# A mixture-of-experts kernel in which four experts are loaded by number, one ring slot is left free for the routed order, and the second pair of experts runs as group 12 of 22

## The chip, the cores and the metric

The kernel runs on one core of a Trainium2 chip. Its time is the device time in microseconds of one execution, and the figure that stands for it is the median of several runs. Five engines work beside each other: TensorE (PE in the profile, with PEld for its weight loads), VectorE (DVE), ScalarE (ACT), GpSimd (POOL) and SyncE (SP), which here issues nearly all loads from memory. They wait for one another by counting semaphores.

## The reference, cut to what matters

A network of two layers works on 256 tokens of width 1024, in float32. The first layer mixes the tokens by attention and a state space model, the second by a long convolution. Each ends in the same mixture of experts, which is the stage that the change touches:

```
def moe(h, router_w, router_b, w_gate, w_up, w_down, sh_gate, sh_up, sh_down):
    scores = jax.nn.sigmoid(jnp.einsum('td,de->te', xf, router_w, preferred_element_type=jnp.float32))
    _, idx = lax.top_k(scores + router_b.astype(jnp.float32), TOP_K)
    sel = jnp.take_along_axis(scores, idx, axis=-1)
    wts = sel / jnp.sum(sel, axis=-1, keepdims=True) * ROUTE_SCALE
    ...
        hid = jax.nn.silu(xb @ w_gate[e]) * (xb @ w_up[e])
        return (hid @ w_down[e]) * w[:, None].astype(xb.dtype)
    ...
    shared = (jax.nn.silu(xf @ sh_gate) * (xf @ sh_up)) @ sh_down
    return (routed + shared).reshape(B, L, Dm)
```

There are 64 experts, each with an inner width of 256; every token goes to its 6 best ones. An expert's weights are 3 MB: 2 MB of gate and up, 1 MB of down. The shared expert, as large as one of the others, sees all tokens. So a layer reads 65 x 3 MB of expert weights, whatever the routing.

## The kernel before

**Columns and groups.** The 64 experts of a layer are worked through in an order that the router computes on the chip, by how many tokens each expert got. A place in this order is a *column*. Columns are put together in 22 groups (`NG`). A group is a pair, two experts of up to 64 tokens each, or a triple, one of up to 64 and two of up to 32. The rows of a group fill the 128 partitions. Groups 0 and 1 are pairs, groups 2 to 21 triples. The code counts triples by `t = n - 2` (`TRIPLES` is 20). What goes beyond these places is done by a loop at the end, which isn't entered here.

**Experts by number.** The order is known only when the router's logits, the choice of six and the counts are through. So that weights can be loaded meanwhile, five experts (`FIXED = STATIC + 1`) stand in columns 0 to 4 by number, whatever their load: DVE overwrites their place in the ranking. `first_experts` loads them ahead of the order.

**The ring.** SBUF holds six slots of 3 MB (`RING`). Column c uses slot `(c + 3) % 6` (`slot_of`), so the slot of column c is freed by the group of column c - 6 (`group_of`). Slot 2 (`SHARED`) first holds the shared expert, and column 5 takes it over. The down weights of columns 5 and 11 go to a tile of their own (`down_aside`).

**Loads.** `moe_loads` (line 570) is SyncE's program for a stage. SyncE waits for the first `tables_ready`, reads expert numbers out of the order table (`expert_at`, line 577), and issues loads (`load`, line 507), each behind a wait on the slot. The semaphores are `sh_gu` (shared expert's gate and up products, one count for each half of them), `gu_front` (the first half of a group's gate and up products), `gu_mm` (all of them) and `dn_mm` (the down products). SyncE issues in program order, so a wait holds back every later load. Loads come in three forms:

- pieces of 1 MB (front half of gate and up, back half, down) for triples 0, 1, 2 and the last,
- gate and up in one load, then down, for triples 3 to 7 and 18 (group 20),
- whole experts of 3 MB for triples 8 to 17:

```
            def whole(t):

                return LATE <= t < TRIPLES - 2
```

A whole expert waits for `dn_mm`; its gate and up can't come ahead of its down weights.

**The work on PE.** `moe_pe` first turns out the logits, then the routing's small matmuls with the shared expert's gate and up products between them (`shared_gate_up(0)` to `(3)`), and then the loop over the 22 groups. A group is: gate and up products (`gate_up_of`), scatter of the group before (`filler`), picking of the next group's rows (`pick_rows`), transposition, down products (`down_of`). Down products signal `dn_mm`, which frees the group's slots. The group's gate and up products wait for its loads. In the profile these matmuls have line 778, that of a helper. Matmuls of 128 x 512 float32 are gate and up or down products, those of 128 x 256 bfloat16 the scatter.

**The order on DVE.** The order table is evicted from PSUM by one operation (line 2011) that needs the second count of `route_mm`. That count is put on the last of three matmuls, of which only the first writes the order.

Of the kernel before, what the change touches and what calls it, by code (L numbers as in the profile page):

```python
# [38 lines left out]
FIXED = STATIC + 1  # L39
PAIRS = STATIC // 2  # L40
NG = PAIRS + (NE - STATIC) // 3
BIG = STATIC + NG - PAIRS
TRIPLES = NG - PAIRS
# [47 lines left out]
def columns_of(n):  # L91

    if n < PAIRS:
        return [(2 * n, slice(0, S)), (2 * n + 1, slice(S, 2 * S))]
    c = STATIC + 3 * (n - PAIRS)
    return [(c, slice(0, S)), (c + 1, slice(S, S + HALF)), (c + 2, slice(S + HALF, 2 * S))]
# [7 lines left out]
def group_of(c):  # L104
    return c // 2 if c < STATIC else PAIRS + (c - STATIC) // 3

# [19 lines left out]
def program(nc, A):  # L126
# [8 lines left out]
    with ExitStack() as ctx:  # L135
# [182 lines left out]

        def w_down(slot, f, c):
            a = 2 * KD * FF + f * D + c * 512  # L320
            return wring[:, slot, a:a + 512]

        def down_aside(c):

            return c % RING == SHARED + RING - FIRST_SLOT and c < 2 * RING
# [5 lines left out]
        def slot_of(e):  # L331
            return (e + FIRST_SLOT) % RING

        def whole(t):

            return LATE <= t < TRIPLES - 2

        def picked_ahead(n):

            return LATE < n - PAIRS < TRIPLES - 1  # L340

        def split_gate_up(c):

            return RING <= c < STATIC + 9

        def down_loads(t, li):

            def loads(last):
                return sum(0 if whole(i) else 2 if i == 0 else 3 for i in range(t % 2, last + 1, 2))
            return li * loads(TRIPLES - 1) + loads(t)  # L350

        def triple_loads(t, li):

            def loads(last):
                return sum(2 if split_gate_up(c) else 1 for i in range(t % 2, last + 1, 2)
                           for c in range(STATIC + 3 * i, STATIC + 3 * i + 3) if c >= FIXED)
            return li * loads(TRIPLES - 1) + loads(t)

# [146 lines left out]
        def _(sp):  # L505
# [54 lines left out]

            def first_experts(li, experts):
                for e in experts:
                    load(wring[:, slot_of(e)], A["w_experts"][li, e], f"w_pair{min(e // 2, 1)}")
# [6 lines left out]
            def moe_loads(li):  # L570
# [3 lines left out]
                first_experts(li, (3, 4))  # L574
# [6 lines left out]
                def gate_up_part(columns, experts, t, front):  # L581
                    for c in columns:
                        n = group_of(c - RING)
# [5 lines left out]
                        name = "w_back" if t == TRIPLES - 1 and not front else f"w_gu{t % 2}"  # L589
                        load(wring[:, slot_of(c), part], A["w_experts"][li, experts[c]][:, part], name)  # L590

                def half_loads(columns, experts, t, down):
                    part, name = (slice(GUW, WEXP), f"w_dn{t % 2}") if down else (slice(0, GUW), f"w_gu{t % 2}")
                    for c in columns:
                        if c - RING >= 0:
                            sp.wait_ge(sem("dn_mm" if down else "gu_mm"), li * (DOWNS if down else NG) + group_of(c - RING) + 1)
                        else:
                            sp.wait_ge(sem("sh_gu"), 2 * (li + 1))
                        if down and down_aside(c - RING) and not down_aside(c):
# [6 lines left out]
                for front in (True, False):  # L606
                    gate_up_part((6,), first, 0, front)
                    gate_up_part((7,), first, 1, front)
                half_loads((6,), first, 0, True)
                half_loads((7,), first, 1, True)  # L610
                gate_up_part((8, 9), first, 1, True)
                gate_up_part((8, 9), first, 1, False)
                half_loads((8, 9), first, 1, True)
                for t in range(2, NG - PAIRS):
                    triple = range(STATIC + 3 * t, STATIC + 3 * t + 3)
                    experts = {c: expert_at(c) for c in triple}
                    if t in (2, TRIPLES - 1):
                        gate_up_part(triple, experts, t, True)
                        gate_up_part(triple, experts, t, False)
                        half_loads(triple, experts, t, True)  # L620
                        continue
                    if whole(t):
                        for c in triple:
                            sp.wait_ge(sem("dn_mm"), li * DOWNS + group_of(c - RING) + 1)
                            load(wring[:, slot_of(c)], A["w_experts"][li, experts[c]], f"w_gu{t % 2}")
                        continue
                    half_loads(triple, experts, t, False)
                    half_loads(triple, experts, t, True)
# [14 lines left out]
            load(wring[:, SHARED], A["w_shared"][0], "w_shared")  # L643
# [42 lines left out]
            load(wring[:, SHARED], A["w_shared"][1], "w_shared")  # L686
# [89 lines left out]
        def _(pe):  # L776
# [316 lines left out]
            def moe_pe(li):  # L1093
# [59 lines left out]
                pe.wait_ge(sem("w_shared"), 16 * (li + 1))  # L1153
                def shared_gate_up(c, ks=range(KD)):
                    for k in ks:
                        last = mm(ps[:, 6 + c // 2, (c % 2) * L:(c % 2 + 1) * L], gate_up(SHARED, k)[:, c * P:(c + 1) * P], hX[:, k], k == 0, k == KD - 1)
# [31 lines left out]
                mm(ps[0:1, 2, 2 * P:2 * P + NE], mcst("tok", 0, 1), sorting[:, 0:NE], True, True)  # L1188
# [3 lines left out]
                last.then_inc(sem("route_mm"), 1)  # L1192
                pe.wait_ge(sem("route"), 4 * (li + 1))
# [10 lines left out]
                def shared_part(n, last):  # L1204

                    ks = ((0,), (1,)) if n == 0 else ((2, 3), (4,)) if n == 3 else ((5, 6), (7,)) if n == 4 else ((), ())
# [5 lines left out]
                for n in range(NG):  # L1212
                    t = n - PAIRS
# [4 lines left out]
                    if t < 0:  # L1218
                        pe.wait_ge(sem(f"w_pair{n}"), 16 * (2, 3)[n] * (li + 1))
                    else:  # L1220
# [463 lines left out]
        def _(dve):  # L1684
# [258 lines left out]
            def moe_dve(li):  # L1943
# [5 lines left out]
                ch(dve.tensor_copy(rank_at[:, 0:STATIC], mcst("iota", 0, STATIC)))  # L1949
                placed = rank_at[:, STATIC:].rearrange("p (g m) -> p g m", m=3)  # L1950
                ch(dve.tensor_copy(placed[:, :, 0], mcst("iota", STATIC, BIG - STATIC)))
# [35 lines left out]
                dve.wait_ge(sem("route_mm"), 3 * li + 1)  # L1987
# [5 lines left out]
                ch(ts(loads[:, 0:FIXED], mcst("iota", 0, FIXED), -1.0, 1e6, M, AD))  # L1993
# [8 lines left out]

                ch(tt(ahead, counts, folded, M))
# [6 lines left out]
                dve.wait_ge(sem("route_mm"), 3 * li + 2)  # L2010
                ch.then(ts(order, ps[0:1, 2, 2 * P:2 * P + NE], -1.0, None, AD), "tables_ready")
                by_rank = ps[:, 2, 0:2 * P].rearrange("p (t n) -> p t n", t=2)
                ch(dve.tensor_copy(pos, by_rank[:, :, 0:NE]))
                ch(dve.tensor_copy(rt[:, :, :, 1], by_rank[:, :, NE:]))

# [3 lines left out]
                def one_hots(q):  # L2019
                    a, b = max(SG * q, PAIRS), min(SG * (q + 1), NG)  # L2020
                    if q == 0:
                        ch(tt(selg[:, :, 0:PAIRS].rearrange("p t g (h s) -> p t (g h) s", h=2), mcst("iota").unsqueeze(1).unsqueeze(1).broadcast_to([P, 2, STATIC, S]),
                              pos[:, :, 0:STATIC].unsqueeze(3).broadcast_to([P, 2, STATIC, S]), ALU.is_equal))
# [9 lines left out]
                def tables(q):  # L2033
# [6 lines left out]
                    if a < PAIRS:  # L2040
                        ch(dve.tensor_reduce(wtab[S + HALF:, a:PAIRS], tab[S + HALF:, 0:PAIRS - a, NR + 1:2 * NR], AX.X, AD))
                    t = max(a, PAIRS)
                    ch.then(dve.tensor_reduce(wtab[S + HALF:, t:b], tab[S + HALF:, t - a:, 2 * NR + 1:3 * NR], AX.X, AD), "tables_ready")

                def hot_columns(n):

                    c = columns_of(n)[0][0]
                    if n < PAIRS:
                        tt(hot[n % 2].rearrange("p t (h s) -> p t h s", h=2), mcst("iota").unsqueeze(1).unsqueeze(1).broadcast_to([P, 2, 2, S]),
                           pos[:, :, c:c + 2].unsqueeze(3).broadcast_to([P, 2, 2, S]), ALU.is_equal).then_inc(sem("hot_ready"), 1)  # L2050
                        return
                    ch(tt(hot[n % 2][:, :, 0:S], mcst("iota").unsqueeze(1).broadcast_to([P, 2, S]), pos[:, :, c:c + 1].broadcast_to([P, 2, S]), ALU.is_equal))
                    tt(hot[n % 2][:, :, S:].rearrange("p t (h s) -> p t h s", h=2), mcst("iota", 0, HALF).unsqueeze(1).unsqueeze(1).broadcast_to([P, 2, 2, HALF]),
# [385 lines left out]
```

## Time and profile before

| | us |
|---|---|
| median of 3 runs | 1430.07 |
| lowest and highest of them | 1428.53, 1432.94 |
| profiled execution, its own time | 1428.19 |
| its span from the first to the last instruction | 1426.3 |
| PE busy in the span | 1270.1 (89%) |
| DVE busy | 610.4 (43%) |
| ACT busy | 273.4 (19%) |

The span is 1.9 shorter than the execution's own time, since that also holds what lies around the instructions. Times in the rows below count from the span's start. Queue 1, which carries nearly all loads, had packets under way for 87.0% of what 16 DMA engines could have had. In the rows, an engine's busy time says that it had an instruction in work, not that it was at its peak. A wait ends with the one that released it, given behind an arrow.

### The profile page before, as it was taken

To read this page: it belongs to the slowest core of one execution; us is meant where nothing else is said; L and a number is where in the kernel's file an instruction comes from. 1 tells how busy PE (TensorE), PEld (TensorE's weight loads), DVE (VectorE), ACT (ScalarE), POOL (GpSimd) and SP (SyncE) were. 2 spreads that over 40 slices of the span, in tenths; PEclk is the share of its full clock that TensorE was granted. 3 is DMA by queue.
4 is the path that set the end of the run, shared out by engine and by line. 5 is a ranking of instruction groups with operands and counts; after the bars stand their busy time and mean duration, and the time that the engine had idled before them with its cause. 6 is when DMAs were issued, how large, how long until landed. Compare 5 with 4: busy or idle time off the path is not lost.

```text
span 1426.3 us, 23074 instructions
## 1 busy us (share of the span) xinstructions
PE 1270.1 (89%) x9704; PEld 729.9 (51%) x9704; DVE 610.4 (43%) x1131; ACT 273.4 (19%) x464; POOL 60.2 (4%) x112
## 2 busy tenths in 40 slices
PE   5999988999998878888899999999999778978887
PEld 1445435775554444454446767875555334443444
DVE  5898872254432222222224687863433212221222
ACT  3226341321111111111112113131111101110111
POOL 0010581000000000000000000000000000000000
PEclk9999999999999999999998999999999989999999
DMA  9664775969999999999998962588999999999996
GB/s 379 230 215 89 161 203 208 411 252 397 422 425 420 428 428 428 427 428 428 425 418 310 380 263 102 227 347 332 397 423 422 421 431 424 425 429 429 421 421 274
DMA packets 53899, 502.84 MB, mean 353 GB/s; under 512 B 9692, under 2 KB 16604, under 8 KB 20188
## 3 DMA queue, kind: packets, MB, share of 16 engines
q1 hardware_dynamic: 53244, 499.18, 87.0%
q8 instruction: 80, 1.31, 0.4%
q10 hardware_dynamic: 544, 2.10, 0.4%
q14 instruction: 31, 0.25, 0.1%
HBM read 496.57 MB, written 4.69 MB: 351 GB/s over the span
## 4 chain that ended last, share of the span: by engine, by line
PE 52%; DMA 35%; DVE 9%; SPq 2%; issue 1%; ACT 1%; DVEq 0%; ACTq 0%
PE ps L778 49%; DMA arena<-in_w_experts 29%; DMA arena<-in_ada_w 6%; SPq L507 2%; PE ps L460 2%; ACT arena L1436 1%; DVE arena L2248 1%; DVE arena L2238 1%; DVE arena L2237 1%; DVE arena L2156 0%; DVE arena L1889 0%; PE ps L831 0%; DVE arena L2236 0%; DVE arena L1902 0%; PE ps L1043 0%
## 5 line engine op out<-in xcount | busy, mean ns | idle before, releaser
L778 PE MATMUL ps<-arena 128*32 128x512 f32 (+10 forms) x9192 | 1214.3, 456 | 138.4 <-DMA arena<-in_w_experts 55.8
L778 PEld LDWEIGHTS ps<-arena 128*32 128x32 f32 (+6 forms) x9192 | 698.5, 139 | 642.9 <-issue 492.1
L1436 ACT ACTIVATE arena<-ps 128x512 f32<-128x512 f32 (+6 forms) x261 | 142.1, 544 | 932.4 <-PE ps L778 886.2
L2098 DVE SCALAR_TENSOR_TENSOR arena<-arena,ps 128x256 f32<-128x256 f32 x44 | 21.1, 481 | 270.0 <-ACT arena L1436 270.0
L1436 ACT ACTIVATE arena<-arena 128x256 f32<-128x256 f32 (+7 forms) x143 | 93.8, 681 | 154.1 <-DVE arena L2116 58.2
L2114 DVE CAST arena<-ps 128x512 bf16<-128x512 f32 x42 | 29.0, 691 | 164.0 <-PE ps L778 164.0
L2058 DVE COPY arena<-ps 128x512 f32<-128x512 f32 x44 | 30.4, 691 | 138.7 <-PE ps L778 138.7
L2086 DVE TENSOR_TENSOR arena<-arena 128x1024 bf16<-128x1024 f32 x42 | 51.5, 1225 | 37.3 <-ACT arena L1436 37.0
L2116 DVE TENSOR_TENSOR arena<-ps,arena 128x1024 f32<-128x1024 f32 x42 | 51.4, 1224 | 1.4
L768 POOL MEMSET arena<- 128x1 f32 x2 | 0.2, 100 | 1168.4 <-PE ps L778 1168.4
L460 PE MATMUL ps<-arena 128*24 128x512 f32 x256 | 33.0, 614 | 3.2 <-DMA arena<-in_ada_w 3.2
L2106 DVE COPY arena<-ps 128x256 f32<-128x256 f32 x44 | 18.5, 422 | 28.6 <-PE ps L1096 28.6
L1436 ACT ACT_TABLE_LOAD x15 | 19.2, 1283 | 23.5 <-DVE arena L2170 11.5
L1436 ACT ACTIVATE arena<-ps,arena 128x512 f32<-128x512 f32 (+3 forms) x29 | 17.0, 585 | 35.2 <-DVE arena L1903 20.6
L2248 DVE SCALAR_TENSOR_TENSOR arena<-arena 128x512 f32<-128x512 f32 x28 | 21.1, 752 | 1.0
L1043 PE MATMUL ps<-arena 128*128 128x128 f32 x64 | 11.0, 299 | 8.4 <-DVE arena L1908 8.2
L1043 PEld LDWEIGHTS ps<-arena 128*128 128x128 f32 x64 | 8.0, 151 | 19.0 <-DVE arena L1908 15.4
L460 PEld LDWEIGHTS ps<-arena 128*24 128x24 f32 x256 | 6.5, 104 | 21.3 <-issue 16.0
L2094 DVE TENSOR_SCALAR arena<-arena 128x256 bf16<-128x256 f32 (+1 forms) x44 | 15.2, 346 | 0.1
L1902 DVE TENSOR_REDUCE arena<-ps 128x1 f32<-128x512 f32 x16 | 11.1, 691 | 8.1 <-PE ps L778 7.8
L2236 DVE TENSOR_SCALAR arena<-arena 128x256 f32<-128x256 f32 x20 | 8.3, 414 | 12.2 <-ACT arena L1436 11.5
L725 POOL TENSOR_TENSOR arena<-arena 128x64 f32<-128x64 f32 (+4 forms) x20 | 10.4, 518 | 57.9 <-ACT arena L1436 56.4
(233 smaller groups left out, 471.6 us busy)
## 6 DMA issues: line engine op xcount, KB each, us to landing
arena<-in_w_experts SPq DMA_DIRECT2D x70, 3072.0 KB, 22.2
arena<-in_w_experts SPq DMA_DIRECT2D x98, 1024.0 KB, 15.0
arena<-in_w_experts SPq DMA_DIRECT2D x38, 2048.0 KB, 21.6
arena<-in_ada_w SPq DMA_DIRECT2D x34, 1024.0 KB, 6.7
arena<-in_ada_w SPq DMA_DIRECT2D x7, 2048.0 KB, 19.4
arena<-in_hy_w_in SPq DMA_DIRECT2D x6, 2048.0 KB, 15.1
arena<-in_w_shared SPq DMA_DIRECT2D x2, 3072.0 KB, 10.5
arena<-in_hy_w_out SPq DMA_DIRECT2D x1, 4096.0 KB, 12.1
```

What stands on the lines that cost most here:

```text
L460: last = pe.matmul(ps[32 * k:32 * k + 2 * GROUP, 7, :], scz[:, 4 * half + k, a:a + 2 * GROUP], w[:, k], start=i == first and half == 0, st ...
L507: sp.dma_start(dst, src).then_inc(sem(name), 16)
L778: return pe.matmul(out, lhsT, rhs, start=start, stop=stop, skip_group_check=skip)
L1043: last = pe.transpose(ps[:, 2 + n % 2, k * P:(k + 1) * P], prob[:, n % 3, k * P:(k + 1) * P], ident)
L1436: return act.activation(out, in_, func, **kw)
L2058: dve.tensor_copy(xgT[n % 2][:, 4:8].rearrange("p k t -> p (k t)"), ps[:, DN + 1, :]).then_inc(sem("xt_dve"), 1)
L2086: tt(yb[:, 2], yr, yb[:, 1], SU).then_inc(sem("y_dve"), 1)
L2098: stt(hh, sg, wtab[:, n:n + 1], ps[:, GU, FF:2 * FF], M, M).then_inc(sem("h_done"), 1)
L2106: dve.tensor_copy(hT2.rearrange("p f t -> p (f t)"), ps[:, HT, 0:2 * P]).then_inc(sem("hT_ready"), 1)
L2114: ch(dve.tensor_copy(yb[:, 0, 0:512], ps[:, DN, :]))
L2116: tt(yr, ps[:, DN:DN + 2, :].rearrange("p b n -> p (b n)"), yb[:, 0], SU).then_inc(sem("y_dve"), 1)
L2248: ins = ts(ada_sums[n], w, c, None, M) if half == 0 and k == 0 else stt(ada_sums[n], w, c, ada_sums[n], M, AD)
```

## The change

Four experts stand by number instead of five, and they stand in columns 0, 1, 2 and 5. Column 3, the first by order, has slot 1, which nothing occupies; column 4 takes over the shared expert's slot, and does so in two halves. Group 0 is a pair, groups 1 to 11 are triples, group 12 (`MIDDLE`) is the second pair (columns 62 and 63), groups 13 to 21 are triples again. `t = n - 1` now counts all groups behind the first, so `LAST` is 20. The slots follow from a table, and `FREED_BY` says which group was the last to use a column's slot.

The shared expert's gate and up arrive as two loads, so that the first two quarters of its products use one half of the slot and the others the second; each partition reads its rows in runs of 256 elements. Its products behind the routing are put in another order, and parts of its down products move to groups 2 and 3. The order table is evicted as soon as its own matmul is through. `whole` now goes up to the last group but one.

The core of the diff:

```diff
-FIXED = STATIC + 1
-PAIRS = STATIC // 2
-NG = PAIRS + (NE - STATIC) // 3
+FIXED_COLUMNS = (0, 1, 2, 5)
+TRIPLES = (NE - 4) // 3
+NG = TRIPLES + 2
+LAST = TRIPLES
+MIDDLE = 12
...
+def slots_of(n):
+
+    if n in (0, MIDDLE):
+        return (FIRST_SLOT, FIRST_SLOT + 1) if n == 0 else (0, FIRST_SLOT)
+    if n < MIDDLE:
+        return (0, 3, 4) if n % 2 == 0 else (5, 1, SHARED)
+    return (0, 3, 1) if n % 2 == 0 else (5, 4, SHARED)
+
+
+SLOT, GROUP_OF, FREED_BY = {}, {}, {}
+for n in range(NG):
+    for slot, (c, _) in zip(slots_of(n), columns_of(n)):
+        FREED_BY[c] = max((GROUP_OF[b] for b in SLOT if SLOT[b] == slot), default=None)
+        SLOT[c], GROUP_OF[c] = slot, n
...
-            return LATE <= t < TRIPLES - 2
+            return LATE <= t < LAST
...
+            def shared_load(li):
+                halves = A["w_shared"][li][:, 0:2 * KD * FF].rearrange("p (k h n) -> p h k n", k=KD, h=2)
+                for h in range(2):
+                    load(wring[:, SHARED, h * KD * FF:(h + 1) * KD * FF].rearrange("p (k n) -> p k n", n=FF), halves[:, h], "w_shared")
+                load(wring[:, SHARED, 2 * KD * FF:], A["w_shared"][li][:, 2 * KD * FF:], "w_shared")
...
-                first_experts(li, (3, 4))
+                first_experts(li, (3,))
...
-                first = {c: expert_at(c) for c in range(FIXED, STATIC + 6)}
-                half_loads((5,), first, 0, False)
-                half_loads((5,), first, 0, True)
...
+                first = {3: expert_at(3)}
+                half_loads((3,), first, 0, False)
+                first[4] = expert_at(4)
+                half_loads((3,), first, 0, True)
+                for n, part in enumerate((slice(0, FRONT), slice(FRONT, GUW))):
+                    sp.wait_ge(sem("sh_gu"), 2 * li + n + 1)
+                    load(wring[:, SHARED, part], A["w_experts"][li, first[4]][:, part], "w_gu0")
+                half_loads((4,), first, 0, True)
+                for t in range(1, LAST + 1):
+                    columns = [c for c, _ in columns_of(t + 1) if c not in FIXED_COLUMNS]
+                    experts = {c: expert_at(c) for c in columns}
+                    if t in (1, 2, 3, LAST):
...
             sp.wait_ge(sem("y_mm"), 1)
-            load(wring[:, SHARED], A["w_shared"][0], "w_shared")
+            shared_load(0)
...
-                mm(ps[0:1, 2, 2 * P:2 * P + NE], mcst("tok", 0, 1), sorting[:, 0:NE], True, True)
+                mm(ps[0:1, GU, 0:NE], mcst("tok", 0, 1), sorting[:, 0:NE], True, True).then_inc(sem("route_mm"), 1)
...
-                shared_gate_up(2)
                 pick_rows(0)
+                shared_gate_up(3, range(0, 4))
+                shared_gate_up(3, range(4, KD)).then_inc(sem("sh_gu"), 1)
                 find_tokens(0)
-                shared_gate_up(3).then_inc(sem("sh_gu"), 1)
...
+                dve.wait_ge(sem("route_mm"), 4 * li + 2)
+                ch.then(ts(order, ps[0:1, GU, 0:NE], -1.0, None, AD), "tables_ready")
+                dve.wait_ge(sem("route_mm"), 4 * li + 3)
```

Three places in the order of instructions. The first is SyncE's program in the first layer, from the router's last constants (`in_mcst`) to the first loads by order. A row gives the line, the operation, what is written and read, and the semaphore waited for; `ISA` carries a wait or the address, `TENSOR_LOAD` reads an entry of the order. Before:

```order
L507 DMA arena<-in_mcst 128x389
L507 DMA arena<-in_w_experts 128x6144 x2
L577 TENSOR_LOAD arena [waits tables_ready]
...
L577 TENSOR_LOAD arena
L577 ISA x2
L507 ISA [waits sh_gu]
L507 DMA arena<-in_w_experts 128x4096
L507 ISA [waits sh_gu]
L507 DMA arena<-in_w_experts 128x2048
L507 ISA [waits gu_front]
```

Now:

```order
L526 DMA arena<-in_mcst 128x389
L526 DMA arena<-in_w_experts 128x6144
L602 TENSOR_LOAD arena [waits tables_ready]
L602 ISA x2
L526 ISA
L526 DMA arena<-in_w_experts 128x4096
L602 TENSOR_LOAD arena
L602 ISA x2
L526 ISA
L526 DMA arena<-in_w_experts 128x2048
L526 ISA [waits sh_gu]
L526 DMA arena<-in_w_experts 128x2048
```

Before, five entries are read and then `sh_gu` stands ahead of the first load; now one entry is read and the 2 MB load behind it has no wait but the table's. The `sh_gu` wait stands two loads later.

The second place is again SyncE's program, at the loads of group 20, the last but one of the stage, three experts. Before:

```order
L507 ISA [waits gu_mm]
L507 DMA arena<-in_w_experts 128x4096
L507 ISA [waits gu_mm]
L507 DMA arena<-in_w_experts 128x4096
L507 ISA [waits gu_mm]
L507 DMA arena<-in_w_experts 128x4096
L507 ISA [waits dn_mm]
L507 DMA arena<-in_w_experts 128x2048
```

Now:

```order
L526 ISA [waits dn_mm]
L526 DMA arena<-in_w_experts 128x6144
L526 ISA [waits dn_mm]
L526 DMA arena<-in_w_experts 128x6144
L526 ISA [waits dn_mm]
L526 DMA arena<-in_w_experts 128x6144
```

Three loads of gate and up ahead of three of down have become three of whole experts, which wait for the down products of the group before in their slots. The third place is DVE's program from the sorting matrix (64 x 64) to the copies of the token places (128 x 128). Before:

```order
L2000 TENSOR_SCALAR arena<-arena 64x64 [waits dve_chain] x2
L2003 TENSOR_TENSOR arena<-ps,arena 128x64 [waits route]
...
L2008 TENSOR_TENSOR arena<-arena 128x1 [waits dve_chain]
L2011 TENSOR_SCALAR arena<-ps 1x64 [waits route_mm,route]
L2013 COPY arena<-ps 128x128 [waits tables_ready]
```

Now:

```order
L2023 TENSOR_SCALAR arena<-arena 64x64 [waits dve_chain] x2
L2030 TENSOR_TENSOR arena<-arena 128x256 [waits route]
L2039 TENSOR_SCALAR arena<-ps 1x64 [waits route_mm]
L2042 COPY arena<-ps 128x128 [waits route_mm,tables_ready]
```

The order's eviction (1 x 64) now comes ahead of the operations on counts, and a selection for group 0 (128 x 256) stands ahead of it.

## Rows read from the trace of the kernel before

**Rows 1.** The page: GB/s in 40 equal slices of the span

```profile
GB/s 379 230 215 89 161 203 208 411 252 397 422 425 420 428 428 428 427 428 428 425 418 310 380 263 102 227 347 332 397 423 422 421 431 424 425 429 429 421 421 274
```

**Rows 2.** Windows: us, busy PE, PEld, DVE, ACT, POOL, PEclk, DMA share, GB/s

```profile
960.00:968.00 8.00, 8.00 (x60) 7.45 (x60) 5.65 (x17) 0.60 (x1) 0.00 (x0) 1.00 0.00 0
444.00:754.00 310.00, 261.43 (x2176) 136.99 (x2173) 76.09 (x124) 36.92 (x57) 0.10 (x1) 0.94 1.00 426
```

**Rows 3.** The page: the chain that ended last, by engine

```profile
PE 52%; DMA 35%; DVE 9%; SPq 2%; issue 1%; ACT 1%; DVEq 0%; ACTq 0%
```

**Rows 4.** SyncE: order reads (durations in ns, starts in us) and first ordered loads

```profile
L577 SPq TENSOR_LOAD <-arena x5: 261/273/485, 299.9 to 302.4; - x5
...
310.96 0.37 SPq L507 DMA_DIRECT2D arena<-in_w_experts  x1
...
968.60 0.35 SPq L507 DMA_DIRECT2D arena<-in_w_experts  x1
```

**Rows 5.** Timeline around the order: start, duration, instruction, [idle before <-releaser]

```profile
298.66 0.09 PEld L778 LDWEIGHTS ps<-arena 128*1 128x1 f32 x2 [0.33 <-issue]
...
299.68 0.21 DVE L2011 TENSOR_SCALAR arena<-ps 1x64 uint32<-1x64 f32 x1 [0.66 <-PE ps L778]
```

**Rows 6.** The chain that ended last: start, duration, step

```profile
592.09 30.22 DMA arena<-in_w_experts
...
637.70 28.68 DMA arena<-in_w_experts
...
1341.96 27.30 DMA arena<-in_w_experts
...
1383.23 1.46 SPq L507
...
1387.07 26.95 DMA arena<-in_w_experts
```

**Rows 7.** Loads issued at 318.50, 344.98 and 327.39; issue to landing

```profile
arena<-in_w_experts SPq DMA_DIRECT2D x1, 1024.0 KB, 13.7
...
arena<-in_w_experts SPq DMA_DIRECT2D x1, 1024.0 KB, 5.6
...
327.39 0.33 SPq L507 DMA_DIRECT2D arena<-in_w_experts  x1
...
arena<-in_w_shared SPq DMA_DIRECT2D x2, 3072.0 KB, 10.5
```

**Rows 8.** PE's timeline, end of the first layer's stage

```profile
725.21 12.96 PE L778 MATMUL ps<-arena 128*32 128x512 f32 x116 [0.86 <-DMA arena<-in_w_experts]
738.11 7.83 PE L778 MATMUL ps<-arena 128*128 128x256 bf16 x70
...
748.56 7.64 PE L778 MATMUL ps<-arena 128*32 128x512 f32 x52 [2.61 <-DMA arena<-in_w_experts]
756.14 8.04 PE L778 MATMUL ps<-arena 128*128 128x256 bf16 x54
```

**Rows 9.** PE's timeline, end of the second layer's stage

```profile
1369.31 9.39 PE L778 MATMUL ps<-arena 128*32 128x512 f32 x84 [0.94 <-DMA arena<-in_w_experts]
...
1414.16 7.29 PE L778 MATMUL ps<-arena 128*32 128x512 f32 x48 [0.88 <-DMA arena<-in_w_experts]
```

**Rows 10.** Windows (columns as in rows 2) and PE's timeline at 1169.81

```profile
748.60:753.90 5.30, 5.30 (x33) 1.30 (x34) 0.00 (x0) 0.00 (x0) 0.00 (x0) 0.68 1.03 428
1169.80:1179.60 9.80, 9.79 (x65) 2.42 (x66) 0.00 (x0) 0.00 (x0) 0.00 (x0) 0.72 0.98 415
...
1169.81 12.11 PE L778 MATMUL ps<-arena 128*32 128x512 f32 x84 [7.17 <-DMA arena<-in_w_experts]
```

**Rows 11.** Window (columns as in rows 2) over the load of w_in

```profile
32.00:38.00 6.00, 4.30 (x28) 1.61 (x26) 4.50 (x2) 0.60 (x1) 0.00 (x0) 1.00 1.05 380
```

**Rows 12.** The router's constants (issued at 277.86; KB, us to landing), first routing product

```profile
arena<-in_mcst SPq DMA_DIRECT2D x1, 194.5 KB, 4.1
...
282.21 3.98 PE L778 MATMUL ps<-arena 128*64 128x256 f32 x16 [1.34 <-ACT arena L1436]
```

More of the change, by code:

```diff
@@ L329, in w_down_of, with slot_of @@
             return at(a, 512) if down_aside(c) else w_down(slot_of(c), f, half)
-        def slot_of(e):
-            return (e + FIRST_SLOT) % RING
+        def slot_of(c):
+            return SLOT[c]
         def whole(t):
-            return LATE <= t < TRIPLES - 2
+            return LATE <= t < LAST
         def picked_ahead(n):
-            return LATE < n - PAIRS < TRIPLES - 1
+            return LATE < n - 1 < LAST
         def split_gate_up(c):
-            return RING <= c < STATIC + 9
+            return c == 4 or RING <= c < 14
         def down_loads(t, li):
             def loads(last):
-                return sum(0 if whole(i) else 2 if i == 0 else 3 for i in range(t % 2, last + 1, 2))
-            return li * loads(TRIPLES - 1) + loads(t)
+                return sum(0 if whole(i) else 2 if i < 2 else 3 for i in range(t % 2, last + 1, 2))
+            return li * loads(LAST - t % 2) + loads(t)
         def triple_loads(t, li):
@@ L355, in loads @@
                 return sum(2 if split_gate_up(c) else 1 for i in range(t % 2, last + 1, 2)
-                           for c in range(STATIC + 3 * i, STATIC + 3 * i + 3) if c >= FIXED)
-            return li * loads(TRIPLES - 1) + loads(t)
+                           for c, _ in columns_of(i + 1) if c not in FIXED_COLUMNS)
+            return li * loads(LAST - t % 2) + loads(t)
         TABLES = 1 + NSETS
@@ L594, in half_loads @@
                     for c in columns:
[L595 to L599, printed above, removed]
+                        if FREED_BY[c] is not None:
+                            sp.wait_ge(sem("dn_mm" if down else "gu_mm"), li * (DOWNS if down else NG) + FREED_BY[c] + 1)
+                        if down and c == 4 + 2 * RING:
                             sp.wait_ge(sem("sh_down"), li + 1)
@@ L611, in moe_loads @@
[L611 to L620, printed above, removed]
+                first = {3: expert_at(3)}
@@ new lines, in moe_loads @@
+                half_loads((3,), first, 0, False)
[9 more added lines that the diff above has]
+                    if t in (1, 2, 3, LAST):
+                        gate_up_part(columns, experts, t, True)
+                        gate_up_part(columns, experts, t, False)
+                        half_loads(columns, experts, t, True)
@@ L621, in moe_loads @@
                         continue
                     if whole(t):
-                        for c in triple:
-                            sp.wait_ge(sem("dn_mm"), li * DOWNS + group_of(c - RING) + 1)
+                        for c in columns:
+                            sp.wait_ge(sem("dn_mm"), li * DOWNS + FREED_BY[c] + 1)
                             load(wring[:, slot_of(c)], A["w_experts"][li, experts[c]], f"w_gu{t % 2}")
                         continue
-                    half_loads(triple, experts, t, False)
@@ L628, in moe_loads @@
-                    half_loads(triple, experts, t, True)
+                    half_loads(columns, experts, t, False)
+                    half_loads(columns, experts, t, True)
                 if li == 0:
@@ L685, in _ @@
             sp.wait_ge(sem("hy_proj"), 6)
-            load(wring[:, SHARED], A["w_shared"][1], "w_shared")
+            shared_load(1)
             sp.wait_ge(sem("filter_mm"), 14 + 1)
```

106 lines of the change are left out of this document (53 added, 53 removed).

## The prediction

> **What bounds the kernel now.** I read first the page's slices of the span: two long stretches move 415 to 430 GB/s in every slice, with holes before and between them [rows 1]. These stretches are the two mixture-of-experts stages, one for each layer. A window over the later part of the first gives a DMA share of 1.00 at 426 GB/s, and one over 8 us near the start of the second gives 0.00 at 0 GB/s, with TensorE busy throughout [rows 2]. The reader is to see both: the queue of expert weights is full for nearly the whole stage, but stands still for some 11 to 13 us while the routing finds out which experts come in which order. The chain that ended last gives 52% to PE and 35% to DMA [rows 3]. That doesn't make PE the bound: PE works at the head of a stage on experts that are there already, and catches the loads up later. What counts is when the queue starts again after the routing, how many bytes come then, where it runs dry, and how long the engines work on after the last bytes.
>
> Then SyncE, which issues the loads. Its five reads of the order table begin at 299.9 and end by 303, but the first load by order goes out only at 310.96, and at 968.60 in the second layer [rows 4]: it waits there for the shared expert's gate and up products to be through with their ring slot, the only one that comes free.
>
> **The restart comes earlier.** The changed kernel leaves slot 1 empty, so column 3 waits for the order alone. The order itself is evicted after its own small matmul, whose weight load starts at 298.66, instead of after the two behind it; today the eviction starts at 299.68 and takes 0.21 [rows 5]. I take 299.05 + 0.21 for the new one, so 299.3. SyncE then reads one entry, not five: from 299.9 the five need until 302.4 plus a last one's 0.5, so one costs about 0.85 with the wake-up, and address arithmetic 0.15. The first load goes out at 300.3 instead of 310.96: 10.7 us earlier. On the vector engine only one operation of 0.4 us is put ahead of the order, and it runs while PE still has that matmul to do. The second layer runs the same instructions; I carry 10.7 over.
>
> **One more expert comes after it.** Only four experts are loaded by number, so 60 instead of 59 follow the restart in each layer. Whole experts land 44.1 us for six apart (622.31 to 666.38 on the chain) [rows 6], 7.35 each: +7.35. Ahead of the restart the missing load saves nothing: the queue only stands still sooner.
>
> **Where the queue runs dry.** At the head, 7 MB are free to go today before SyncE has to wait for the down products of group 0; the seventh, issued at 318.5, lands 13.7 later at 332.2, that is 21.2 after the restart. After the change 10 MB are free to go (columns 3 and 4, and gate and up of columns 6 and 7): 7.5 more, so they land by 329.0. The next piece waits for the down products of group 0, which PE, with the same work ahead, ends as today: the load that they release goes out at 327.39. A 1 MB piece issued into an empty queue lands 5.6 after its issue [rows 7], so at 333.0, where an unbroken queue would land it at 331.5. That is 1.5 lost; today the piece issued at 344.98 found an empty queue too, and lost about 0.9. Net +0.6. The second half of the shared expert's slot may cost another 0.1 to 0.5; I keep that for the range.
>
> In the middle there is a new one. Group 12 is now the pair of columns 62 and 63, and group 13 takes slots 5, 4 and 2 in that order. Slot 5 is freed by the down products of group 11, so SyncE waits for these with slot 4 long free behind it. From the landing of a whole group to the issue that its down products release it is 14.0 us (1369.26 to 1383.23) [rows 6], and a 3 MB load into an empty queue lands 10.5 after its issue [rows 7]: 24.5. The queue holds only the pair by then, so unbroken it would land that load after 2 x 7.35 + 7.35 = 22.05. +2.4. With triples in flight the queue holds 22 us of work, and the same wait costs nothing.
>
> Group 20 is now loaded in whole experts, no longer gate and up first. Eighteen MB in pieces took 44.76 (1369.26 to 1414.02) where six whole ones take 44.07 [rows 6], so 9 MB gain 0.35. The last byte therefore lands, per layer, -10.7 + 7.35 + 0.6 + 2.4 - 0.35 = -0.7 us.
>
> **The end of each stage.** This is the largest term. Today PE starts group 20's gate and up as soon as their 6 MB are there, with 12 MB still to come: 725.21. From there it needs 20.73 to the end of the first half of group 21 (738.11 + 7.83), then waits 2.61 for the second half, and from 748.56 needs 15.62 to the last product at 764.18 [rows 8]. The last byte lands 7.5 after 748.5, at 756.0: PE ends 8.2 behind it. In the second layer the last byte lands at 1414.02, and PE ends at 1421.45 [rows 9], 7.4 behind. After the change group 20 can't start until all 9 of its MB are there, with only the 9 MB of group 21 to come, 22.5 us of queue. PE needs 20.73 + 15.62 = 36.35 from there and has no wait left in it: it ends 13.9 behind the last byte. The tails grow by 5.7 and 6.5: +12.2.
>
> The clock belongs to this. The 15.62 contains a stretch at 1.2 GHz (granted clock 0.68 over 748.6 to 753.9, after 2.6 us of idling). After the change that idling goes, but there are 22.0 - 14 = 8 us of idling ahead of group 20's gate and up; after 7.17 us of it the same products took 9.8 us at 0.72, and with what follows 12.11 [rows 10] against 9.39 [rows 9]. I let the one slow stretch stand for the other. Without any it would be 1.7 less per layer, by 1169.81 1.0 more.
>
> **The shared expert's pieces.** Its gate and up are fetched in runs of 1 KB. The nearest row is that of the 1.6 KB runs of w_in, 380 GB/s [rows 11], against 426 for expert weights [rows 2]: 0.28 us per MB more for 631 runs, so with 1024 runs 0.5 per MB, 1.0 for two. In the first layer this pushes the whole queue back, and the router's constants, which stand at its end, land 4.1 after their issue at 277.9 [rows 12], 0.2 ahead of the first routing product at 282.2. So the routing moves by nearly all of it: +1.0, bounds 0 and 3 (runs cost three times more than I drew). In the second layer the queue is idle then. By the Trainium skill ("DMA: Bandwidth & Descriptors", Specifications) runs of 512 B and more go at line rate, so 1 KB runs would cost nothing and the sum would be 1.0 less. The row doesn't bear the rule out at 1.6 KB.
>
> **Sum.** 1.0 + 2 x (-0.7) + 12.2 = +11.8, on the profiled execution's 1428.2 us: 1440.0. That execution is 1.9 below the median of the runs, which gives 1430.1 + 11.8 = **1441.9**. The rest (order of small vector operations, one more semaphore, shared down products one group earlier) lies behind PE's 25 us without a gap and ahead of waits with over 0.5 us of slack; if that cover failed at the last table products, 0.5 us per layer.
>
> **Rivals.** (1) *The last byte decides.* If PE could hide group 20 behind the last 9 MB, the tail would stay and only -1.4 + 1.0 be left: 1429.7. For it: the queue's full share in every window. Against: 36.35 us of work behind 22.5 us of queue; it decides from 30.9 down. (2) *Faster: the bytes decide alone.* If the queue, once started, never waits for a slot, restart against expert is -10.7 + 7.35 - 0.35 per layer, and with the tail hidden 1423.7. The place is the slot waits, 3.0 a layer by the sum above; it wins if PE frees slots some 3 us earlier than the rows say. (3) *It doesn't do what it says:* the restart still waits for something at 310, and both layers lose the extra expert on top: about 1463. Against: the order of issue has no wait but the table there. (4) *Slower still:* slow stretches add up in group 11 and in both tails and the 1 KB runs cost 3: 1448 to 1452.
>
> **Numbers.** The measurement tells this kernel from itself to about 0.3%, 4.3 us. Forecast as worked out, 1436 to 1447: 0.68; rival 1: 0.12; rival 2: 0.10; rival 3: 0.02; rival 4: 0.08. Faster 0.10, same 0.12, slower 0.78. The range for 8 in 10 reaches down to the upper part of rival 1 and up into rival 4: 1431 to 1448.
>
> **What would show it.** First ordered load at about 301 and 10.7 earlier than today in the second layer; one gap of 2 to 4 us in the queue when group 12's pair has landed; group 20's gate and up starting 22.5 before the last byte; PE ending 12 to 15 behind the last byte. Wrong would make me: a tail of 8, a queue without the middle gap, or 1 KB runs that push the first layer's routing by more than 3.

## The result

The changed kernel takes 1445.5 us in the median of four runs (1444.4 to 1446.8), the kernel before on the same chip 1429.7 (also four). The ratio is 1.0112, with a 95% interval of 1.0091 to 1.0132: slower by 15.9 us. Forecast were +11.8 and 1441.9, with a range of 1431 to 1448.

The profiled execution of the changed kernel took 1446.75 us, the longest of its four; its span is 1444.9, against 1426.3 before. So the two profiles differ by 18.6, some 2.7 more than the medians. The parts below are those of the profiles. First the page of the changed kernel, slices of the span and the chain that ended last:

```profile
GB/s 384 243 195 80 168 226 203 408 284 400 420 423 421 430 426 383 427 429 427 429 401 250 399 228 86 248 307 384 418 424 422 425 430 365 426 431 427 430 421 192
...
PE 55%; DMA 33%; DVE 8%; issue 1%; SPq 1%; ACT 1%; DVEq 0%; ACTq 0%
```

Against [rows 1] either stage has a dent that wasn't there, 383 in slice 16 and 365 in slice 34, and the last slice has 192 instead of 274: the span goes on longer after the loads. PE's share of the chain is up from 52% to 55%.

**The restart.** SyncE's timeline: the first loads by order in either layer, and the load into the second half of the shared expert's slot; then VectorE's eviction of the order in the first layer.

```profile
301.03 0.36 SPq L526 DMA_DIRECT2D arena<-in_w_experts  x1
...
311.48 0.33 SPq L526 DMA_DIRECT2D arena<-in_w_experts  x1
...
967.35 0.35 SPq L526 DMA_DIRECT2D arena<-in_w_experts  x1
...
299.79 0.21 DVE L2039 TENSOR_SCALAR arena<-ps 1x64 uint32<-1x64 f32 x1 [0.76 <-PE ps L799]
```

Against [rows 4] the first layer's queue restarts 9.9 us earlier. In the second layer SyncE starts to read the order at 966.44 and issues 0.9 later, where it was 11.1 before: 10.15 earlier. The order itself is there 0.1 later than in [rows 5], not 0.6 earlier.

**The middle.** Windows around group 13's first load in the second layer (columns as in rows 2):

```profile
1214.00:1219.00 5.00, 5.00 (x47) 2.99 (x43) 1.40 (x4) 0.38 (x1) 0.00 (x0) 1.00 0.71 305
1219.00:1224.00 5.00, 2.88 (x28) 0.97 (x21) 1.92 (x2) 1.09 (x2) 0.00 (x0) 1.00 0.35 93
1224.00:1229.00 5.00, 5.00 (x47) 3.74 (x49) 2.18 (x3) 1.17 (x2) 0.00 (x0) 1.00 1.02 433
```

That load on SyncE's timeline, in the first and the second layer:

```profile
553.48 0.33 SPq L526 DMA_DIRECT2D arena<-in_w_experts  x1
...
1221.68 0.33 SPq L526 DMA_DIRECT2D arena<-in_w_experts  x1
```

And its size and its time from issue to landing, again in the first and the second layer:

```profile
arena<-in_w_experts SPq DMA_DIRECT2D x1, 3072.0 KB, 10.2
...
arena<-in_w_experts SPq DMA_DIRECT2D x1, 3072.0 KB, 11.2
```

The reader is to see a queue that falls to 93 GB/s for five microseconds and is full again behind them. It thins out before it stops: the window ahead has only 305 GB/s at a share of 0.71, although the pair's last expert landed at 1220.62. The next load was issued 1.06 after this landing. It landed at 1232.91, 12.3 behind the one before it instead of 7.35: 4.95 lost. In the first layer the issue came 0.66 before the pair's last landing; that load and the one behind it lost 2.15 and 0.94.

**The tails.** PE's timeline at the end of the first and of the second layer's stage:

```profile
734.63 14.95 PE L799 MATMUL ps<-arena 128*32 128x512 f32 x116 [5.51 <-DMA arena<-in_w_experts]
749.42 0.27 PE L1117 MATMUL ps<-arena 128*128 128x128 f32 x1
749.53 13.57 PE L799 MATMUL ps<-arena 128*128 128x256 bf16 x122
762.94 0.27 PE L1117 MATMUL ps<-arena 128*128 128x128 f32 x1
763.05 8.04 PE L799 MATMUL ps<-arena 128*128 128x256 bf16 x54
...
1402.93 15.30 PE L799 MATMUL ps<-arena 128*32 128x512 f32 x116 [6.85 <-DMA arena<-in_w_experts]
...
1431.70 8.04 PE L799 MATMUL ps<-arena 128*128 128x256 bf16 x54
```

The stage's last load, issued at 730.35 and at 1397.31, with its time to landing:

```profile
arena<-in_w_experts SPq DMA_DIRECT2D x1, 1024.0 KB, 26.8
...
arena<-in_w_experts SPq DMA_DIRECT2D x1, 1024.0 KB, 28.2
```

Group 20 starts only when its third whole expert is there, at 734.6, after 5.51 of idling. From there PE works without a gap to 771.09, 36.5 us. The last byte landed at 757.10 (1425.55 in the second layer), so PE ends 14.0 (14.2) behind it, where [rows 8] and [rows 9] gave 8.2 and 7.4.

### The profile page after: what moved, and what is told of

It reads as the page before. It is cut to its first block, busy times and chain, and to the rows that moved or that the text cites. A ratio compares the mean times of both kernels' runs of the same rounds, so it can differ in the third digit from the quotient of the medians.

```text
span 1444.9 us, 23082 instructions
## 1 busy us (share of the span) xinstructions
PE 1275.3 (88%) x9704; PEld 726.0 (50%) x9704; DVE 610.3 (42%) x1137; ACT 273.5 (19%) x464; POOL 59.9 (4%) x112
## 4 chain that ended last, share of the span: by engine, by line
PE 55%; DMA 33%; DVE 8%; issue 1%; SPq 1%; ACT 1%; DVEq 0%; ACTq 0%
PE ps L799 52%; DMA arena<-in_w_experts 26%; DMA arena<-in_ada_w 7%; PE ps L479 2%; SPq L526 1%; ACT arena L1458 1%; DVE arena L2274 1%; DVE arena L2182 0%; DMA arena<-in_mcst 0%; DVE arena L1911 0%; DVE arena L2264 0%; DVE arena L2263 0%; PE ps L852 0%; DVE arena L1924 0%; PE ps L1064 0%
## 5 line engine op out<-in xcount | busy, mean ns | idle before, releaser
L799 PE MATMUL ps<-arena 128*32 128x512 f32 (+9 forms) x9192 | 1219.2, 460 | 150.4 <-DMA arena<-in_w_experts 63.0
L799 PEld LDWEIGHTS ps<-arena 128*32 128x32 f32 (+5 forms) x9192 | 694.6, 140 | 663.5 <-issue 503.4
L2132 DVE COPY arena<-ps 128x256 f32<-128x256 f32 x44 | 18.6, 422 | 30.9 <-PE ps L1117 30.9
L1924 DVE TENSOR_REDUCE arena<-ps 128x1 f32<-128x512 f32 x16 | 11.1, 692 | 9.2 <-PE ps L799 8.9
L2262 DVE TENSOR_SCALAR arena<-arena 128x256 f32<-128x256 f32 x20 | 8.3, 415 | 13.5 <-ACT arena L1458 12.8
```

Of the source, the lines that this page charges most:

```text
L799: return pe.matmul(out, lhsT, rhs, start=start, stop=stop, skip_group_check=skip)
L2132: dve.tensor_copy(hT2.rearrange("p f t -> p (f t)"), ps[:, HT, 0:2 * P]).then_inc(sem("hT_ready"), 1)
```

## The experiments

All ratios are to the kernel before, measured on the same chip. What "comes back" is the difference of two medians, the changed kernel's 1445.5 and that of the version, from two series of runs; the kernel before had medians of 1429.45 to 1429.8 in all of these.

**Group 20 in halves again.** Does the form of this one load make the tails?

```diff
-                return LATE <= t < LAST
+                return LATE <= t < LAST - 1
```

> The changed kernel, with group 20 loaded gate and up first again. Theory (the tails): group 20's gate and up start with 12 MB still to come, PE ends 7.4 to 8.2 behind the last byte instead of 14.0 and 14.2, so 12.6 come back, less 0.7 for the pieces: about 1433.5 (1431 to 1436). Rival (the tails are longer because one more expert and a later last byte shift PE's work, whatever the form of the load): within 2 of 1445.5.

Measured: 1430.9 in the median, ratio 1.0017 (1.0001 to 1.0033), so 14.6 come back (13.6 by the ratios), somewhat more than the 11.9 of the theory; the time lies just below its range. PE's timeline at the end of its first layer, where the last byte landed at 760.15:

```profile
752.70 5.95 PE L799 MATMUL ps<-arena 128*32 128x512 f32 x52 [1.16 <-DMA arena<-in_w_experts]
...
760.29 7.29 PE L799 MATMUL ps<-arena 128*32 128x512 f32 x48 [0.87 <-DMA arena<-in_w_experts]
```

PE ends 7.4 behind the last byte in both layers. The theory's mechanism holds, the rival falls: the additional expert doesn't lengthen the tail. The gap in the middle is still there (3.2 and 3.3).

**Slot 4 first.** Does the queue's gap behind the pair come from the order of the slots? The load into slot 4 needs a semaphore of its own, since group 11's loads, on the same count, aren't used up yet.

```diff
...
-    return (0, 3, 1) if n % 2 == 0 else (5, 4, SHARED)
+    return (0, 3, 1) if n % 2 == 0 else (4, 5, SHARED)
...
-                            load(wring[:, slot_of(c)], A["w_experts"][li, experts[c]], f"w_gu{t % 2}")
+                            load(wring[:, slot_of(c)], A["w_experts"][li, experts[c]], "w_early" if c == EARLY else f"w_gu{t % 2}")
...
```

> The changed kernel, with slot 4 instead of slot 5 as the first slot of group 13 and of the odd groups behind it; the load into slot 4 has a semaphore of its own. Theory (the queue runs dry behind the pair): the gap of 3.05 in the first layer and of 4.93 in the second goes, the tails stay, so about 8 come back: 1437.5 (1435 to 1440). Rival (what the queue loses there it has as slack further on, or the gap only moves to slot 5's load): within 2 of 1445.5.

Measured: 1439.5, ratio 1.0086 (1.0068 to 1.0105): 6.0 come back by the medians, 3.7 by the ratios, with tails of 13.5 and 13.2. Windows over the two places (columns as in rows 2):

```profile
550.00:560.00 10.00, 7.88 (x72) 4.71 (x68) 4.10 (x5) 2.25 (x3) 0.00 (x0) 1.00 1.00 427
1215.00:1230.00 15.00, 13.04 (x117) 7.64 (x118) 4.97 (x8) 2.54 (x4) 0.00 (x0) 1.00 1.02 433
```

The queue is full through both, and slot 5's load, issued next, finds slot 4's still under way. So the gap came from the order of two slots in a table. The time fell into the theory's range, but the interval overlaps that of the change (1.0091 to 1.0132), so how much end time the gap cost is known only roughly; part of what came back lies in the slightly shorter tails.

**Both edits.**

> The two edits before together. Theory: tails and gap are separate terms and add up: 1445.5 - 12 - 8 = 1425.5 (1422 to 1429), faster than the kernel before by about 4. Rival (they are one loss seen twice, a late PE): no better than the better of the two alone, about 1433.

Measured: 1429.2, ratio 1.0006 (0.9987 to 1.0024): 16.4 come back, no difference to the kernel before. The 1425.5 of the theory isn't reached, and 1429.2 lies just above its range. Alone the edits gave 14.6 and 6.0, but runs of this version spread from 1422 to 1436, so that the medians don't settle whether the two add up. The rival, no better than the better one alone, isn't excluded by them. The trace has both effects side by side. PE's timeline at the end of its second layer:

```profile
1381.60 12.96 PE L800 MATMUL ps<-arena 128*32 128x512 f32 x116 [1.00 <-DMA arena<-in_w_experts]
...
1405.05 7.64 PE L800 MATMUL ps<-arena 128*32 128x512 f32 x52 [2.71 <-DMA arena<-in_w_experts]
...
1412.63 8.04 PE L800 MATMUL ps<-arena 128*128 128x256 bf16 x54
```

The wait for the second half of group 21 is back (2.71 here; 2.61 in the first layer's [rows 8]), the tails are 7.9 and 8.2, and there is no gap in the middle.

**The kernel before with group 20 in whole experts.** The suspected cost put into the other kernel, alone:

```diff
-                return LATE <= t < TRIPLES - 2
+                return LATE <= t < TRIPLES - 1
```

> The kernel before, with group 20 loaded as whole experts and nothing else. Theory: tails grow from 8.2 and 7.4 to 14, less 0.7: 1429.7 + 11.7 = 1441.4 (1439 to 1444), so most of the change's loss is this one bound. Rival (whole experts at the end cost nothing where the stage starts as before): within 2 of 1429.7.

Measured: 1443.7, ratio 1.0109 (1.0093 to 1.0126), +14.2, with tails of 14.6 and 14.4. PE's timeline at the end of its first layer:

```profile
731.22 15.52 PE L778 MATMUL ps<-arena 128*32 128x512 f32 x116 [6.69 <-DMA arena<-in_w_experts]
...
746.69 13.58 PE L778 MATMUL ps<-arena 128*128 128x256 bf16 x122
...
760.21 8.04 PE L778 MATMUL ps<-arena 128*128 128x256 bf16 x54
```

They are the rows of the changed kernel's tail: a wait for the third whole expert, then products without a further wait. This one number in `whole` makes nearly as much as the whole change.

**The restart put back.** The free slot stays, but the first load waits for the shared expert's products again:

```diff
+                sp.wait_ge(sem("sh_gu"), 2 * li + 2)
                 half_loads((3,), first, 0, False)
```

> The changed kernel with one wait more: the first load by order waits for the second half of the shared expert's products, as before the change. Theory (the early restart is real gain while the queue has bytes free to go): the 10 MB that are free land at 338.6 instead of 330.3 in the first layer, about 8 later, and in the second 7.6; the tails stay: 1445.5 + 15.6 = 1461 (1457 to 1465). Rival (the head of the stage is set by PE's down products of group 0 anyway): within 2 of 1445.5.

Measured: 1461.3, ratio 1.0219 (1.0200 to 1.0239), +15.7 on the changed kernel. The first load goes out at 311.65, and the first layer's last byte lands at 766.3 instead of 757.1. So the earlier restart is worth 8 us a layer and not its full 10. The traces show where the rest goes: here the 20th MB behind the restart lands 53.76 and 54.21 after the first issue, in the changed kernel 56.55 and 56.40. With 10 MB free to go, the earlier queue reaches the next waits sooner and loses 2.8 and 2.2 there.

**The shared expert's last products ahead.** In the version with both edits the load into the second half of the shared slot still lost 2.2 in either layer.

```diff
+                shared_gate_up(3, range(0, 4))
+                shared_gate_up(3, range(4, KD)).then_inc(sem("sh_gu"), 1)
                 pick_rows(0)
-                shared_gate_up(3, range(0, 4))
-                shared_gate_up(3, range(4, KD)).then_inc(sem("sh_gu"), 1)
```

> The version with group 20 in halves and slot 4 first, with the shared expert's last products ahead of the picking of group 0's rows, so that its second half comes free some 3.7 earlier. In the version without this the load into that half lost 2.2 in either layer. Theory (behind it stands the wait for the down products of group 0, reached with 2.6 to 3.5 of queue left): most of the 2.2 is lost again there; 0 to 1 per layer remain: 1428.2 (1427 to 1430). Rival (the 2.2 come back in full): 1424.8.

Measured: 1439.6, ratio 1.0069 (1.0051 to 1.0086), 10.4 slower than without the edit. Neither expectation holds. VectorE's and PE's timeline in the first layer:

```profile
314.80 0.69 DVE L2088 COPY arena<-ps 128x512 f32<-128x512 f32 x1 [7.31 <-PE ps L800]
...
317.68 5.63 PE L800 MATMUL ps<-arena 128*128 128x8 bf16 x40 [2.99 <-DVE arena L2069]
```

The loads issued at 323.51 and 336.35, with their time to landing:

```profile
arena<-in_w_experts SPq DMA_DIRECT2D x1, 1024.0 KB, 4.9
...
arena<-in_w_experts SPq DMA_DIRECT2D x1, 1024.0 KB, 5.0
```

VectorE copies the picked rows of group 0 before it builds the one-hot matrices that PE's table products need. It now idles 7.31 for the picking, and PE then idles 2.99 for the matrices. Group 0 comes later, and the loads that its products release find an empty queue (4.9 and 5.0 to landing; behind a queue it would be more). From the restart to the last byte it is 460.2 and 460.3, against 455.5 and 453.6. That wasn't meant, but it shows that a delay of PE's group 0 goes through to the end.

**The same with VectorE in the earlier order.**

```diff
-                picked_rows(0)
                 dve.wait_ge(sem("route_mm"), 4 * (li + 1))
...
                 hot_columns(1)
+                picked_rows(0)
```

> The kernel of the run before with VectorE's copy of the picked rows of group 0 behind the one-hot matrices of the first groups, where the kernel before the change has it, so that PE doesn't wait 3.0 for these. The second half of the shared slot is free some 3.7 earlier, and group 0 ends no later. Theory (the next wait, that for the down products of group 0, takes over): from the restart to the last byte 452.5 to 455.5, against 455.5 and 453.6 without the edit, and 1427 to 1430 in all. Rival (the 2.2 lost at the shared slot come back in full): 451.4 to 453.3, and about 1424.8.

Measured: 1431.2, ratio 1.0013 (0.9998 to 1.0028), above the range of the theory and far from the rival. From restart to last byte 454.8 and 456.0, the second above the theory's range too. The load into the second half goes out at 308.50, in time; the first load that waits for group 0's down products, at 329.47, has only 1.6 of queue left and lands 5.1 after its issue, in the version without the edit 6.8 after it. In the second layer 0.8 is left, and it loses 1.6. SyncE's timeline at 308.50, and the time to landing of the load issued at 329.47:

```profile
308.50 0.33 SPq L527 DMA_DIRECT2D arena<-in_w_experts  x1
```

```profile
arena<-in_w_experts SPq DMA_DIRECT2D x1, 1024.0 KB, 5.1
```

The rival's 2.2 aren't gained in either layer. In the second layer the stall has moved to the next wait, where the version without the edit lost nothing; in the first that version lost 0.9 there too, and what holds the queue up besides isn't shown.

**A free slot alone.** The kernel before with four experts by number, column 4 in the empty slot, column 5 behind the shared expert as ever; the pairs stay where they were.

```diff
-FIXED = STATIC + 1
+FIXED = STATIC
...
-                half_loads((5,), first, 0, False)
-                half_loads((5,), first, 0, True)
+                for c in (4, 5):
+                    half_loads((c,), first, 0, False)
+                    half_loads((c,), first, 0, True)
...
```

> The kernel before with four experts by number, column 4 into the empty slot right behind the order, column 5 behind the shared expert as before. Theory: its 3 MB fit just into the hole up to 310.8, where the queue stands as today, so the restart 10 earlier gains only what the additional expert costs: 1429.5 (1428 to 1432). Rival (restart 10 against expert 7.35 in each layer): 1424.

Measured: 1431.5, ratio 1.0005 (0.9991 to 1.0019). The first load by order goes out 3.7 after the order (six entries are read ahead of it), 7.3 earlier than before, and from there to the last byte it takes 453.1, 8.0 more: the gain is the additional expert's cost, no more.

**The shared expert's pieces in the kernel before.**

```diff
...
-            load(wring[:, SHARED], A["w_shared"][0], "w_shared")
+            shared_load(0)
...
```

> The kernel before with the shared expert's gate and up in the two loads of 1 KB runs, nothing else. Theory: the three loads land 11.2 after the first issue instead of 10.2, the router's constants about 6 after theirs instead of 4.1, and the first routing product waits for them: 1 to 2 more, 1431 (1429.5 to 1432). Rival (runs of 1 KB go at full rate): landing after 10.2 and 4.1, 1429.5.

Measured: 1429.9, ratio 1.0005 (0.9993 to 1.0017). PE's timeline at the first routing product:

```profile
280.92 2.40 PE L789 MATMUL ps<-arena 128*64 128x256 f32 x10 [2.37 <-DMA arena<-in_mcst]
```

The first piece of the shared load (issued at 244.79) and the router's constants (275.03), with their time to landing:

```profile
arena<-in_w_shared SPq DMA_DIRECT2D x1, 1024.0 KB, 5.8
...
arena<-in_mcst SPq DMA_DIRECT2D x1, 194.5 KB, 5.8
```

The steps are those of the theory: all three pieces are there 11.3 after the first issue (10.2 before the change), the constants 5.8 after theirs (4.1), and PE waits 2.37 for these. The end is not: order and stage come 52.6 after the shared load's issue, against 52.3 before, and the time doesn't differ. Between the first routing product and the order PE's granted clock was lower in the profile of before (0.71 over 282 to 292) than here (0.81 over 280 to 290), so one profile against another doesn't settle where the wait was hidden. The interval leaves room for -1.0 to +2.4, so neither the theory nor the rival falls.

## Why the prediction was right, step by step

- **Restart**, -10.7 a layer: measured -9.9 and -10.15. In the first layer the +1.0 of the shared pieces belongs to it, so -9.7 was forecast there: PE's first routing product waited 1.86 for the constants, which took back what the earlier eviction gave.
- **One more expert**, +7.35: the free slot alone shows that restart and expert come out even (7.3 against 8.0).
- **Head**, +0.6: too small. From the first issue to the landing of the 20th MB it takes 56.55 and 56.40, in the kernel before 55.21 and 55.43: +1.3 and +1.0. One row was misread: the piece issued at 344.98 didn't find an empty queue, since the load ahead of it landed at 347.16. Loads that did, in the run with the shared expert's last products ahead, landed 4.9 and 5.0 after their issue, not 5.6; with 5.0 the sum would have given about nothing here. What was priced too low is the second half of the shared slot, at 0.1 to 0.5. In the second layer its load lost 2.2, issued with 2.2 of queue left, and in the version with both edits it lost 2.2 in either layer. In the first layer the queue dips at the same place (352 GB/s over 311 to 315), but the delay of 1.3 falls on the load ahead, and the kernel before has one of 1.1 without this wait. What can be gained there is limited by the wait for group 0's down products, as far as the two runs on the shared products show.
- **Middle**, +2.4 a layer: mechanism and place right, the size too small. It was 3.1 and 4.95. The 14.0 from landing to release [rows 6] held in the first layer; in the second it was 15.7, because group 11's products fell into a stretch at half clock (below).
- **Tails**, +5.7 and +6.5: measured 5.8 and 6.8. The 36.35 us of PE work were 36.5 and 36.8. The idling ahead of it was 5.5 and 6.85, not 8, but the slow stretch came as assumed: group 20's first products took 14.95 and 15.30 instead of 12.96. The run that undoes it and the run that does it alone both confirm the term; it is the largest part of the loss.
- **Group 20's form**, -0.35: the last 18 MB took 44.49 and 44.64, in the kernel before 45.44 and 44.76.
- **Shared pieces**, +1.0: the load takes 1.0 longer as worked out. Whether the time does isn't settled; alone, in the kernel before, it came out between -1.0 and +2.4.
- **Sum**: +11.8 forecast, +15.9 measured. The mis-sized terms are the middle (8.0 for both layers instead of 4.8) and the head (2.3 instead of 1.2). Of the 18.6 between the profiles another 2.0 lie between the first stage and the second routing (193.35 against 195.35). Other profiles, of kernels that don't differ there, have 192.5 to 195.8, so I put this down to the execution and not to the change.

**Rivals.** That the last byte decides fell with the tails. "Faster: the bytes decide alone" fell with the waits at the head: they are PE's, and an earlier start of the queue meets the next of them. Without tails and middle gap the change ends even with the kernel before (1429.2): 10 of restart buy one expert of 7.35, and the head takes part of the rest; where the remainder goes isn't shown. No version that was run beats the kernel before clearly. One that would fill the head's wait with the down weights of column 4 wasn't tried: their place still holds what the shared products read.

## What to carry to other kernels

When a load is made larger at the end of a stream, compare the compute that remains from its landing with the bytes still to come; here 36 us against 22.5 cost 6 us twice. An earlier start of a queue is worth only what can be issued until the next wait: look for the consumer that releases it, and expect the stall to move there. Where a smaller batch stands among larger ones, check which slot the load behind it waits for, while another is free.

## What was unexpected of the hardware

Group 11's gate and up products took 9.39 in the first layer and 11.08 in the second. PE's timeline of both:

```profile
539.55 9.39 PE L799 MATMUL ps<-arena 128*32 128x512 f32 x84 [1.06 <-DMA arena<-in_w_experts]
...
1206.04 11.08 PE L799 MATMUL ps<-arena 128*32 128x512 f32 x84 [2.32 <-DMA arena<-in_w_experts]
```

A window within the latter (columns as in rows 2):

```profile
1206.30:1209.70 3.40, 3.40 (x20) 0.87 (x16) 0.00 (x0) 0.00 (x0) 0.00 (x0) 0.50 1.00 426
```

The granted clock was 0.50, that is 1.2 GHz, for 3.4 us behind 2.32 of idling; behind 1.06 of idling the same products ran at full clock. So the slow stretch cost 1.7, and this made a middle gap of 3 into one of 5. The length of the wait alone doesn't decide it: in the kernel before with group 20 in whole experts, group 19's products follow 2.31 of idling in both layers. Their rows, and windows within them:

```profile
709.14 11.05 PE L778 MATMUL ps<-arena 128*32 128x512 f32 x84 [2.31 <-DMA arena<-in_w_experts]
...
1375.22 9.39 PE L778 MATMUL ps<-arena 128*32 128x512 f32 x84 [2.31 <-DMA arena<-in_w_experts]
...
709.20:712.60 3.40, 3.40 (x20) 0.78 (x24) 0.00 (x0) 0.00 (x0) 0.00 (x0) 0.51 1.00 426
...
1375.30:1384.50 9.20, 9.20 (x85) 3.92 (x86) 0.97 (x3) 0.38 (x1) 0.00 (x0) 1.00 1.00 424
```

In the first layer they began at half clock, in the second at full clock. What made the difference isn't shown.

The runs of 1 KB: by the Trainium skill ("DMA: Bandwidth & Descriptors", Specifications) runs of 512 B and more go at line rate. The three loads, 2 MB of them in 1 KB runs, landed 11.2 after their first issue, the same 3 MB as one load 10.2. The load also became three issues. Windows while it was under way, of the changed kernel and of the kernel before (columns as in rows 2):

```profile
249.50:255.50 6.00, 5.37 (x28) 4.42 (x27) 0.00 (x0) 3.67 (x4) 0.00 (x0) 1.00 1.10 369
...
250.00:256.00 6.00, 5.37 (x27) 4.42 (x26) 0.00 (x0) 3.67 (x4) 0.00 (x0) 1.00 0.99 427
```

The DMA engines are busy throughout in both, but move 369 GB/s instead of 427. At these rates 2 MB take 0.8 longer, so most of the 1.0 goes with the length of the runs and not with gaps between the issues. The rule isn't borne out at 1 KB here.
